# GpSimd lowers the weights of a hybrid decoder step in instructions of one, two or four k-tiles, by stage

## The reference

```
hn = rmsnorm(h)
h  = h + Mixer_i(hn)                       # layer 0: gated DeltaNet (GDN), layer 1: Mamba-2 SSD
h  = h + rmsnorm(p_i @ W_proj) * sigmoid(h @ W_gate)
y  = rmsnorm(h)                            # after both layers

GDN:  qkv, z, a, b = split(hn @ w_in);  qkv = silu(causal_conv(qkv));  q, k = l2norm
      chunked delta rule for the prompt (a triangular inverse in each chunk), a recurrence for the samples
      out = (rmsnorm(o) * silu(z)) @ w_out
SSD:  z, xbc, dt = split(hn @ w_in);  xbc = silu(causal_conv(xbc))
      chunked state space scan, recurrence for the samples
      out = (groupnorm(y * silu(z))) @ w_out
```

## Time and profile before

| | |
|---|---|
| median of 3 runs | 2419.1 us |
| the profiled execution's own time | 2417.6 us |
| its span, first to last instruction | 2415.8 us |
| TensorE busy | 2326.3 us, 96% |
| GpSimd busy | 1794.2 us, 74% |
| VectorE busy | 1614.2 us, 67% |
| ScalarE busy | 1276.5 us, 53% |
| mean granted TensorE clock | 0.990 |

### The profile page before, as it was taken

One profiled execution on the slowest core, in us unless ns is written; L12 is line 12 of the kernel. 1 busy time (PEld: TensorE's weight loads), 2 busy tenths in 40 slices (PEclk: granted clock), 3 DMA queues, 4 the chain that ended last, 5 costly groups with the idle time before them and its releaser, 6 DMA issues.

```text
span 2415.8 us, 59306 instructions
## 1 busy us (share of the span) xinstructions
PE 2326.3 (96%) x21792; PEld 2183.8 (90%) x21792; DVE 1614.2 (67%) x3159; ACT 1276.5 (53%) x2236; POOL 1794.2 (74%) x2284
## 2 busy tenths in 40 slices
PE   5899999999999999999999979999999999999997
PEld 5799999999999999989999978999999999899997
DVE  7667666666666676761217576998999989703375
ACT  4555555555555555543335456555555555433453
POOL 5566566565555556558889968888898889798896
PEclk9999999999999999999999989999999999999999
DMA  5444444444444444436444446766576657454443
GB/s 200 154 155 151 157 155 151 149 150 145 146 154 149 145 144 147 145 125 223 149 167 151 158 148 211 228 202 206 199 245 215 194 196 239 174 195 157 153 156 118
DMA packets 126776, 410.89 MB, mean 170 GB/s; under 512 B 21344, under 2 KB 37984, under 8 KB 122112
## 3 DMA queue, kind: packets, MB, share of 16 engines
q1 hardware_dynamic: 80784, 294.49, 35.2%
q10 hardware_dynamic: 45936, 115.64, 14.1%
HBM read 363.47 MB, written 46.61 MB: 170 GB/s over the span
## 4 chain that ended last, share of the span: by engine, by line
POOL 37%; PE 34%; issue 22%; DVE 4%; ACT 1%; POOLq 0%; DMA 0%; DVEq 0%; ACTq 0%
POOL wl L336 36%; PE psj L381 10%; PE psj L383 10%; PE psj L382 10%; POOL h L344 1%; PE psA L773 1%; PE psE L403 1%; PE psE L747 1%; PE psA L721 1%; DVE h L2012 0%; DVE arena L1535 0%; DVE xl L1819 0%; DVE xl L1460 0%; PE psB L727 0%; ACT xh L845 0%
## 5 line engine op out<-in xcount | busy, mean ns | idle before, releaser
L336 POOL TENSOR_TENSOR wl<-ring,wh 128x256 fp32r<-128x256 f32 x2232 | 1760.9, 824 | 600.4 <-ACT wh L826 599.8
L381 PE MATMUL psj<-xh,wh 128*128 128x288 f32 x4400 | 1357.9, 309 | 31.7 <-DVE xl L1460 16.5
L382 PE MATMUL psj<-xl,wh 128*128 128x288 f32 x4400 | 1305.7, 297 | 0.0
L383 PE MATMUL psj<-xh,wl 128*128 128x288 f32 x4400 | 1301.0, 296 | 0.0
L381 PEld LDWEIGHTS psj<-xh,wh 128*128 128x128 f32 x4400 | 831.3, 189 | 83.1 <-issue 43.9
L826 ACT ACTIVATE wh<-ring 128x1024 fp32r<-128x1024 f32 x558 | 586.5, 1059 | 583.8 <-PE psj L383 535.1
L382 PEld LDWEIGHTS psj<-xl,wh 128*128 128x128 f32 x4400 | 833.7, 189 | 1.9
L383 PEld LDWEIGHTS psj<-xh,wl 128*128 128x128 f32 x4400 | 834.6, 190 | 0.0
L907 ACT ACTIVATE arena<-psj 128x256 f32<-128x256 f32 x112 | 42.7, 381 | 190.7 <-PE psj L383 185.0
L1811 DVE TENSOR_TENSOR h<-h,psj 128x288 f32 x32 | 14.6, 455 | 155.7 <-PE psj L383 155.7
L1885 DVE SCALAR_TENSOR_TENSOR arena<-arena 128x256 f32<-128x256 f32 x144 | 110.7, 796 | 3.4
(11 more groups left out here) (346 smaller groups left out, 2965.4 us busy)
## 6 DMA issues: line engine op xcount, KB each, us to landing
ring<-weights_d SPq DMA_DIRECT2D x558, 512.0 KB, 3.3
h<-gstate_d ACTq DMA_DIRECT2D x16, 1024.0 KB, 6.1
gst_s_d<-h ACTq DMA_DIRECT2D x16, 1024.0 KB, 3.9
h<-sstate_d ACTq DMA_DIRECT2D x32, 512.0 KB, 5.4
sst_s_d<-h ACTq DMA_DIRECT2D x32, 512.0 KB, 5.0
arena<-g_rows_d ACTq DMA_DIRECT2D x16, 864.0 KB, 6.0
arena<-s_rows_d ACTq DMA_DIRECT2D x8, 1152.0 KB, 8.6
h_spill_d<-h ACTq DMA_DIRECT2D x2, 2304.0 KB, 7.5
```

The source lines that it names most:

```text
L336: ins = pool.tensor_tensor(wl[:, s, n:n + 2], ring[:, s, n:n + 2], wh[:, s, n:n + 2].bitcast(F32), ALU.subtract)
L381: pe.matmul(out, w_h, xh[:, kt, :], start=(kt == 0), stop=False)
L382: pe.matmul(out, w_h, xl[:, kt, :], start=False, stop=False)
L383: mm = pe.matmul(out, w_l, xh[:, kt, :], start=False, stop=(kt == KT - 1))
```

## The change

`lower` gets a parameter `step`, the k-tiles of one instruction: 1, 2 or 4. The k-tiles, their order, the waits and the one semaphore increment a half stay as they are. A half is then 8 instructions of 128x128, 4 of 128x256, or 2 of 128x512. GpSimd's GDN loop (halves 12 to 203) uses 1; halves 204 to 295 use 4; 296 to 455 use 2; 456 to 555 use 4; halves 0 to 11 and the last two, 556 and 557, keep 2.

```
-            def lower(count, s):
+            def lower(count, s, step=2):
                 pool.wait_ge(wh_ready, count)
-                for n in range(0, 8, 2):
-                    ins = pool.tensor_tensor(wl[:, s, n:n + 2], ring[:, s, n:n + 2],
-                                             wh[:, s, n:n + 2].bitcast(F32), ALU.subtract)
+                for n in range(0, 8, step):
+                    ins = pool.tensor_tensor(wl[:, s, n:n + step], ring[:, s, n:n + step],
+                                             wh[:, s, n:n + step].bitcast(F32), ALU.subtract)
                 ins.then_inc(wl_ready, 1)
...
             with pool.Fori(0, GH) as m:
                 for k in range(12):
                     hc = 2 * T_GLOOP + k
-                    lower(m * 12 + (hc + 1), hc % 4)
+                    lower(m * 12 + (hc + 1), hc % 4, 1)
...
-            with pool.Fori(0, (N_HALF - at) // 4) as r:
-                for s in range(4):
-                    lower(r * 4 + (at + s + 1), s)
+
+            def rounds(first, end, step):
+
+                with pool.Fori(0, (end - first) // 4) as r:
+                    for s in range(4):
+                        lower(r * 4 + (first + s + 1), s, step)
+
+            to_ssd, to_dense = 2 * T_SPRO // 4 * 4, 2 * (T_SEND + 4) // 4 * 4
+            rounds(at, to_ssd, 4)
+            rounds(to_ssd, to_dense, 2)
+            rounds(to_dense, 4 * N_ROUND, 4)
```

## The result

The changed kernel takes 2435.43 us, the median of 6 runs (2431.78 to 2435.95), beside 2419.42 us before (6 runs, 2417.37 to 2422.41). The ratio is 1.0064, with a 95% interval of 1.0054 to 1.0074: slower by 16 us, outside the range of the prediction. The profiled execution took 2435.95 us (span 2434.1, before 2415.8).

The account below looks back on a forecast made before the run. TensorE's own work plus its stalls was taken as the bound; -4.5 - 0.5 - 0.3 + 2.0 + 2.4 - 0.5 = -1.4 us on the profiled 2417.6 us, against a 2419.1 us median, gave 2417.7 us, range 2408 to 2430.

Parts of the forecast that it names:

- First iteration: First GDN iteration: line 1579's copy waits behind a GpSimd instruction or two; shorter ones give back 0.5 us.
- GDN loop: One k-tile shortens VectorE's waits for GpSimd, so the 15 stalls for line 1618 lose 0.3 us each: -4.5 us.
- C: Rival: GpSimd falls behind in the GDN loop from 0.48 us per one-k-tile instruction; at 0.55 us +37 us, 2455; chance 0.07.
- the masks of line 344: GDN loop: they come 2 us later, TensorE reads them only at the end of the inverse; cost nothing.
- Second x: Output products, once a layer: line 1442 alternates with two four-k-tile instructions a half; +1.0 us, twice, +2.0.
- PLE: PLE stages: one or two of line 1819's eight runs lose 0.5 to 1 us; +1.2 us a stage, +2.4.
- rival B: Long instructions block VectorE in PLE stages and at second x where TensorE waits; +5 to +18 us, some 2428; chance 0.18.
- Gate stages: GpSimd's half falls from 3.3 to about 2.8 us, VectorE ends at most 2.3 us later; nothing gained or lost.
- Behind the gate: GpSimd's backlog gone earlier, line 1852 falls from 0.98 towards 0.5 us before the SSD layer's x: -0.5 us.

Follow-up runs that it names:

- e9: Kernel before with one k-tile in the first round of the GDN loop alone; 2424.15 us, ratio 1.002.
- e1: Kernel before with one k-tile in the GDN loop alone, two everywhere else; 2424.66 us, ratio 1.0025.
- e3: Changed kernel with a pause of GpSimd ahead of its fourth half of each GDN round; 2429.33 us, ratio 1.004.
- e4: Changed kernel with the 16-column copy of line 1587 as a two-input maximum of its input with itself; 2434.21 us, ratio 1.006.
- e5: Changed kernel with all four small copies of a GDN iteration as two-input maxima; 2431.84 us, ratio 1.0046.
- e7: Kernel before with one k-tile in the GDN loop alone, four small copies as two-input maxima, three masks in six half-size instructions; 2421.79 us, ratio 1.0008.
- e8: e7 with one k-tile also beside the PLE stages (halves 260 to 263 and 520 to 527); 2424.13 us, ratio 1.0016.
- e2: Kernel before with four k-tiles in the output, PLE and gate stages alone, two in the GDN loop; 2428.76 us, ratio 1.0037.
- e6: Kernel before with the four small copies of a GDN iteration as two-input maxima; 2420.09 us, ratio 1.0.
- e10: Kernel before with one k-tile in GDN rounds 2 to 16, two in the first round and everywhere else; 2419.83 us, ratio 1.0003.
- e11: e10 with one k-tile also at the second x and PLE stages (halves 228 to 231, 260 to 263, 488 to 495, 520 to 523); 2422.89 us, ratio 1.0011.
- e14: Kernel before, with GpSimd waiting for its own last instruction behind each half of the first GDN round; 2419.56 us, ratio 1.0002.
- e15: Kernel before with four k-tiles in the dense stages, but two at halves 228-231, 260-263, 456-463, 488-495, 520-527; 2423.55 us, ratio 1.0017.
- e12: Kernel before with one k-tile in the GDN loop, GpSimd waiting for its own last result behind each half; 2422.23 us, ratio 1.0012.
- e13: Kernel before with one k-tile in the GDN loop, GpSimd waiting for its own last instruction behind each half of the first round only; 2419.17 us, ratio 1.0001.

## Why the prediction was wrong

*First iteration: "It can give back 0.5 us (ends 0 and -1.4)".* This is the step that failed, in its sign. Measured: +8.1 us of profile in the change, and +5.2 us of median when nothing else is changed (e9). I saw VectorE's copy behind "a GpSimd instruction or two" and concluded that shorter instructions make the wait shorter, for I took it as given that VectorE gets its turn behind the one in flight. That is what the rows of VectorE at work show; the copy comes from rest into a running train, and the one row of that kind, itself, I had not read against GpSimd's timeline. A range whose end was zero for want of a reason against a loss was the fault in the working.

What the runs show in its place: in the profiled executions with one k-tile in an unbroken first round (after, e1, e3, e4, e5, e7, e9, and e8) seven of eight have one VectorE instruction of 3.5 to 10.3 us that ends within 0.05 us of the end of GpSimd's train; with two k-tiles (before, e2, e6, e10, e11, e14, e15) or gaps (e12, e13) none of nine has. Each held one was the first that VectorE started after 2.5 to 8.5 us of rest, as a copy or with two inputs. With instructions of 0.70 us the copy of the earlier trace rows already ended as the train did (88.61 and 88.58 us), and GpSimd had started two more instructions while it waited, at 87.12 and 87.82 us: a short hold was in the profile of before, in a stretch of GpSimd's timeline that I had not asked for.

```profile
85.73 2.85 POOL L336 TENSOR_TENSOR wl<-ring,wh 128x256 fp32r<-128x256 f32 x4
```

In later iterations the same lines take no more than one instruction's rest, and there they start with no idle time of VectorE ahead of them. No instruction of VectorE with all operands in SBUF has more than 1.3 us of rest ahead of it there, in before, the change or e1, so the situation of the hold comes in the first iteration alone.

*GDN loop: -4.5 us.* Measured +1.2 us in the change, -3.1 to -3.2 us in e1, e5, e7, e8 and e10. The undisturbed price of a one-k-tile instruction was right (0.416 us against 0.40), and where the loop gained, shorter rests did remove stalls, some two thirds of what I took. C did not come, but by luck as much as by the working: I had left out that more instructions take turns with VectorE more often. They cost 0.50 to 0.55 us in the burst, over the 0.48 us that I had named as the limit, and 0.2 us of lead was left. What failed beside it is "the masks of line 344 come 5x = 2 us later ... Cost: nothing". I had asked who reads the masks and not whom they block. The masks are 0.73 us long, kept their size, and came 3.5 us later (14.69 instead of 11.17 us after the iteration's first matmul), beside the line in front of 1626: one stall of 0.54 us an iteration in place of 0.46. In the five kernels that gain they stand 0.1 us later still, at 14.79 us; in the change, e3, e4, e11 and e13, which don't, at 14.69 us. The rows show what goes with it. Line 1617 is two small instructions there. In the change both wait for a mask (0.79 and 0.77 us, together 1.49 us); in e1 the first gets in (0.25 us) and only the second waits (0.73 us, together 0.90 us), and TensorE has no stall there. e10 and e11 have the same code in the loop and differ by 3.9 us in this way. No run moved the masks by themselves, so that their place is the cause is argued from the rows; what sets it is not known.

*Second x: +1.0 us each.* Right: by starts the stalls grew from 2.28 to 3.37 us at the first, by the mechanism described, two long instructions in a half. The stage's own +0.8 us (e2 +1.2) lies within what it moves by without an edit.

*PLE: +1.2 us each.* The mechanism was right, rival B's, and the size too small: +2.2 us each. I had followed the eight by assumed starts and found one or two that lose 0.5 to 1 us. By starts three within the stage lost 0.81 to 0.91 us each, where one had lost 0.41 us before: 2.62 - 0.41 = 2.2 us. A fourth stall, ahead of the gate stage's first matmul, was there before too.

*End of the SSD layer: not in the sum.* The first halves of output product 1 are lowered while VectorE ends the SSD layer, which TensorE waits for. Line 2011 holds two operands in SBUF too, and its wait went from 0.4 to 2.1 us; this is 1.7 of the 2.4 us that the stage loses beyond the second x. In e2 (+4.3 us) the wait is 2.1 us too, and in e15 (+2.1 us), with two k-tiles at the second x, still 1.9 us. I had looked at the places where I knew of a wait, and the entry of 0.4 us for that line is not among.

*Gate stages:* right, nothing, though VectorE takes 12 us more. *Behind the gate:* line 1860 fell from 0.98 to 0.51 us as predicted, and the wait for VectorE became one for ScalarE (line 1186, 1.2 us): no gain.

*Sum by stages:* first iteration +8.1, loop +1.2, output product 0 +0.8, PLE +4.4, output product 1 +3.5, behind gate 1 +0.6, all others together -0.3: 18.3 us, the difference of the two spans. Rival B had the right side of the sum, but its terms of 3 to 8 us a PLE stage and 2 to 4 us a second x were larger than the 2.2 and 1.1 us measured, and it had no part in the first iteration. C's "over 160 us" at 0.70 us an instruction does not come out of its own terms (4 x 2.8 - 4.1 = 7.1 us a round, 114 us); nothing rested on it.

The Trainium skill ("SBUF — State Buffer", section "SBUF: two separate sides") says that the shared pair is locked for a whole instruction and the loser blocks. In its part "Who interferes with whom" it says that the order of issue decides and not the shape. Copies and two-input instructions were held alike (e5), which agrees. It lets the loser wait for the winner's instruction; the 10.26 us of line 1587, in which 20 lowerings and 3 masks ran, are more than that rule gives. Its price of 2.6 cycles an element ("GPSIMD Engine Reference", section "3.1 Elementwise — side-by-side cycle accounting") gave estimates of 0.42 and 1.25 us, and the trace agrees with 0.416 and 1.25.

**Open.** Why the train keeps VectorE out in most executions and not in e8's, and why the copy at 84.04 us got in and the one at 87.00 us did not. What spreads e1 (2418.96 to 2429.14 us) and e5 over 5 us and more: only one execution of each was profiled, and a hold that comes and goes does not explain it alone, for e1's profiled one is its fastest and has the hold. Whether e13's gaps of about 0.1 us let the copy in, or only moved its arrival: it started in the middle of a half and not at a gap. What shifts the masks by 0.1 us. Why gate 1 lost 1.6 us in e8 and e15, and the SSD loop 3.15 us in e10.

No version beats the kernel before by more than can be told; e13 (2419.17 beside 2419.32 us) comes nearest.

## What to carry to other kernels

The size of an instruction on an engine that shares SBUF access with VectorE acts on VectorE three ways: its rest is what a busy VectorE waits for, its pauses are where a VectorE that comes from rest and is held gets in at last, and its total moves everything behind it. Before making one engine's instructions shorter and more, look for each place where the other engine comes from rest into an unbroken train of them; before making them longer, list every wait of TensorE for a line with two SBUF operands, the small ones too, and read which instruction is beside it. An estimate that gives a step no bad end needs a row that shows the same situation, here rest and train, not just the same two engines.

## What the runs showed of the hardware

- One VectorE instruction of 128x16 took 10.26 us beside a train of 20 GpSimd instructions of 0.42 us and 3 of 0.7 us, and ended 0.03 us behind the train. Seven of eight profiled executions with an unbroken train of one-k-tile instructions had such a hold (3.5 to 10.3 us). It took a copy and a two-input instruction alike.
- Two-input GpSimd instructions on 128 partitions, start to start: 0.416 us for 128 columns, 0.70 for 256, 1.25 for 512. The first two give 0.13 us fixed and 0.57 us for each 256 columns.
- A GpSimd instruction that waits for the semaphore of the one ahead of it starts 0.16 us late (e12), which was enough for 15 new waits of TensorE where the ring of four halves had 0.2 us of lead left. Beside VectorE's work in the GDN burst the 128x128 instruction took 0.50 to 0.55 us instead of 0.416.
